# Differential attention in a four-layer kernel: mixing a head's two attention maps before the transpose instead of mixing its two outputs after the product with the values

## The reference, cut to what matters

```python
def diff_attention(h, cos, sin, w_qkv, q_norm, k_norm, lam_p, subln, w_o, layer_idx):
    ...
    lam = jnp.exp(jnp.sum(lp[0] * lp[1])) - jnp.exp(jnp.sum(lp[2] * lp[3])) + lambda_init
    ...
        s = jnp.einsum('bqhcd,bkhcd->bhcqk', qblk, k).astype(jnp.float32) * scale
        causal = kpos[None, :] <= qpos[:, None]
        p = jax.nn.softmax(jnp.where(causal, s, NEG_INF), axis=-1)
        a = p[:, :, 0] - lam * p[:, :, 1]
        return jnp.einsum('bhqk,bkhe->bqhe', a.astype(v.dtype), v)
    ...
    o = rms_norm_2(o, subln) * (1.0 - lambda_init)
    return o.reshape(B, S, DA_V) @ w_o
```

## Time and profile before

| what | value |
|---|---|
| timed runs, median | 1524.88 us (1522.94 to 1527.48) |
| profiled execution | 1526.05 us |
| its span in the trace | 1524.3 us |
| mean granted clock of TensorE, 1 is 2.4 GHz | 0.981 |
| PE busy | 1437.7 us, 94% of the span |
| DVE busy | 939.1 us, 62% |
| ACT busy | 741.4 us, 49% |
| third mixer's attention, first scores to first product of the output projection | 980.07 to 1014.53 us |

### The profile page before, as it was taken

How to read it: one execution, slowest core, us unless ns; L and a number is a source line. 1 busy time by engine, 2 the same in 40 slices (tenths; PEclk the granted TensorE clock), 3 DMA queues, 4 the chain that set the end, 5 groups by cost and what they waited for, 6 DMA issues and landing times.

```text
span 1524.3 us, 19988 instructions
## 1 busy us (share of the span) xinstructions
PE 1437.7 (94%) x7838; PEld 1222.0 (80%) x7838; DVE 939.1 (62%) x1653; ACT 741.4 (49%) x1252; POOL 17.2 (1%) x43
## 2 busy tenths in 40 slices
PE   2889989898999999999999999999999998999998
PEld 2878979887888888888888878778888876888887
DVE  3766666675665554675655559977555487565553
ACT  4734352433444444554545446655444365554441
POOL 2200000000000000000000000000000000000000
PEclk9999999999999999999999999999999997999999
DMA  7413222220456555452665545406655551165552
GB/s 215 111 42 84 83 70 70 69 71 29 142 168 201 181 192 181 147 170 83 200 187 182 191 156 176 166 15 208 190 182 189 186 172 62 56 208 186 187 189 88
DMA packets 168092, 216.60 MB, mean 142 GB/s; under 512 B 10993, under 2 KB 136256, under 8 KB 167872
## 3 DMA queue, kind: packets, MB, share of 16 engines
q1 hardware_dynamic: 166816, 213.03, 43.6%
q10 hardware_dynamic: 1184, 2.31, 0.4%
HBM read 214.26 MB, written 1.05 MB: 141 GB/s over the span
## 4 chain that ended last, share of the span: by engine, by line
PE 84%; DVE 10%; ACT 2%; DMA 2%; issue 1%; POOL 1%; ACTq 0%; SPq 0%; DVEq 0%; POOLq 0%
PE psum L881 22%; PE psum L883 22%; PE psum L882 22%; PE psum L1116 3%; PE psum L1111 2%; DVE w_low L628 2%; PE psum L1227 2%; PE psum L1069 2%; PE psum L1203 2%; DVE work L2187 1%; PE psum L1164 1%; PE psum L1051 1%; DMA ring<-in_gdn_w_in 1%; PE psum L1216 1%; PE psum L661 1%
## 5 line engine op out<-in xcount | busy, mean ns | idle before, releaser
L628 DVE TENSOR_TENSOR w_low<-ring,w_high 128x1024 fp32r<-128x1024 f32 (+3 forms) x395 | 473.7, 1210 | 341.5 <-ACT w_high L614 339.8
L614 ACT ACTIVATE w_high<-ring 128x1024 fp32r<-128x1024 f32 (+3 forms) x395 | 410.6, 1049 | 460.4 <-PE psum L883 443.7
L881 PE MATMUL psum<-w_high,hT 128*128 128x512 f32 (+2 forms) x944 | 373.0, 395 | 0.6 <-DVE hT L1997 0.6
L883 PE MATMUL psum<-w_high,hT 128*128 128x512 f32 (+2 forms) x944 | 367.1, 389 | 0.0
L882 PE MATMUL psum<-w_low,hT 128*128 128x512 f32 (+2 forms) x944 | 366.4, 388 | 0.0
L881 PE MATMUL psum<-w_high,parts 128*128 128x512 f32 (+1 forms) x532 | 208.2, 391 | 1.3 <-ACT arena L1681 1.3
L883 PEld LDWEIGHTS psum<-w_high,hT 128*128 128x128 f32 x944 | 177.8, 188 | 36.8
L883 PE MATMUL psum<-w_high,parts 128*128 128x512 f32 (+1 forms) x532 | 206.2, 388 | 0.0
L881 PEld LDWEIGHTS psum<-w_high,hT 128*128 128x128 f32 x944 | 178.2, 189 | 34.8 <-DVE hT L1997 0.9
L882 PE MATMUL psum<-w_low,parts 128*128 128x512 f32 (+1 forms) x532 | 206.0, 387 | 0.0
L882 PEld LDWEIGHTS psum<-w_low,hT 128*128 128x128 f32 x944 | 178.3, 189 | 34.1
(11 more groups left out here) (278 smaller groups left out, 1541.0 us busy)
## 6 DMA issues: line engine op xcount, KB each, us to landing
ring<-in_ffn_w_gate_up SPq DMA_DIRECT2D x176, 256.0 KB, 3.1
ring<-in_w_gate_up SPq DMA_DIRECT2D x176, 256.0 KB, 3.1
ring<-in_gdn_w_in SPq DMA_DIRECT2D x48, 512.0 KB, 4.0
ring<-in_ffn_w_down SPq DMA_DIRECT2D x44, 512.0 KB, 3.2
ring<-in_w_down SPq DMA_DIRECT2D x44, 512.0 KB, 3.2
ring<-in_da_w_qkv SPq DMA_DIRECT2D x24, 512.0 KB, 3.8
ring<-in_gdn_w_out SPq DMA_DIRECT2D x16, 512.0 KB, 3.3
ring<-in_mla_w_out SPq DMA_DIRECT2D x8, 512.0 KB, 3.9
```

Of the source, the lines that this page charges most:

```text
L614: nc.scalar.activation(piece_slot(w_high, n), piece_slot(ring, n), ACT.Copy).then_inc(s.w_hi, 1)
L628: nc.vector.tensor_tensor(piece_slot(w_low, n), piece_slot(ring, n), piece_slot(w_high, n).bitcast(F32), ALU.subtract).then_inc(s.w_lo, 1)
L881: mm(out, lhs[0], rhs[0], start=start, stop=False)
L883: return mm(out, lhs[1], rhs[0], start=False, stop=stop)
```

## The change

The two maps of a head are combined before they are turned. With `e0`, `e1` the exponentials and `s0`, `s1` their row sums, DVE writes `e0 + (-lambda * s0 / s1) * e1` over `e0`. PE turns that one map (three transposes in place of six) and multiplies it by the values once (three products of width 128 in place of six of width 129). DVE scales the output by `1 / s0`. The row sums no longer come from a column of ones; they are accumulated by the exponentials on ACT (`accum_out`).

The order changes too. On PE a round is: scores of `i + 2` (which wait for the exponentials of `i`), transposes of `i` (which wait for the new signal `mixed`), values of `i - 1`. Transposes alternate between banks 4 and 5, outputs between banks 6 and 7, so `values(i)` waits for the end of round `i - 2`. On ACT a round is: exponentials of `i + 1`, one copy of the turned map, then the squares of head `i - 2` (the piece's `split_high` in round 0). On DVE: `mix(i)`, maxima of `i + 2`, `finished(i - 1)`; `split_low` stands in front of `mix(1)` and `output_norm(0)` in front of `mix(6)`. For heads 0 to 5 the squares are one instruction without a sum, and `output_norm` sums them on DVE: heads 0 to 3 in one reduction over 128x1024, heads 4 and 5 in one over 128x512.

```diff
             def difference_attention(A, q, k, v, outs):      # PE, new
+                def values(i):
+                    if i >= 2:
+                        pe.wait_ge(A.end, i - 1)
+                    pe.wait_ge(A.pT, i + 1)
+                    for t in range(T):
+                        for kt in range(t + 1):
+                            last = mm(B[6 + i % 2][:, t * P:(t + 1) * P], at_pT[:, i % 2, (t + kt) * P:(t + kt + 1) * P], v(i, kt),
+                                      start=(kt == 0), stop=(kt == t))
+                    last.then_inc(A.o_psum, 1)
...
+                for i in range(A.rounds):
+                    if i + 2 < A.rounds:
+                        pe.wait_ge(A.exps, 2 * i + 2)
+                        masked_scores(A, q, k, i + 2)
+                    elif i == A.rounds - 1:
+                        turned_out(0)
+                        turned_out(1)
+                    pe.wait_ge(A.mixed, i + 1)
+                    if i >= 2:
+                        pe.wait_ge(A.pT, i - 1)
+                    for n in range(3):
+                        last = nc.tensor.transpose(B[4 + i % 2][:, n * P:(n + 1) * P], at_s[:, i % 2, 0, n * P:(n + 1) * P], ident)
+                    last.then_inc(A.pT_psum, 1)
+                    if i:
+                        values(i - 1)
+                values(A.rounds - 1)
...
+            def difference_attention(A):                     # ACT, new
...
+                            last = f(at_s[:, u, j, keys_of(t)], B[2 * u + j][:, keys_of(t)], ACT.Exp, scale=A.scale,
+                                     bias=nmax[u][:, t, j:j + 1], accum_out=esum[u][:, t, j:j + 1])
...
+                exps(0)
+                for i in range(A.rounds):
+                    if i + 1 < A.rounds:
+                        exps(i + 1)
+                    act.wait_ge(A.pT_psum, i + 1)
+                    if i >= 2:
+                        act.wait_ge(A.o_psum, i - 1)
+                    f(at_pT[:, i % 2, :], B[4 + i % 2][:, 0:3 * P], ACT.Copy).then_inc(A.pT, 1)
+                    if i == 0:
+                        split_high(act, a_da + 23 + SPLIT)
+                    elif i >= 2:
+                        output_squares(i - 2)
...
-            v.memset(d_v[:, :, :, P:P + 1], 1.0)
...
-            def da_write(i, outs, e):
-                own(ts(e[:, :, 1], e[:, :, 1], lam[:, 3:4], None, ALU.mult))
-                own.wait()
-                own(tt(at_maps, outs, per_map(e, P), ALU.mult))
-                own.wait()
-                return tt(at_o[:, :, i * P:(i + 1) * P], at_maps[:, :, 0, :], at_maps[:, :, 1, :], ALU.add)
             def output_norm(b):
...
+                dve.wait_ge(s.out_sq, 4 if b == 0 else 6)
...
+                own(v.reduce_sum(by_head_t, da_sq[:, summed, :, :].rearrange("p h t n -> p t h n"), AX_X))
+                own.wait()
...
+            def difference_attention(A, turned):             # DVE, new
+                def mix(i):
+                    u = i % 2
+                    dve.wait_ge(A.exps, 2 * i + 2)
+                    if i >= 4:
+                        dve.wait_ge(A.end, i - 3)
+                    own(v.reciprocal(parts_of[i % 4], esum[u]))
+                    own.wait()
+                    own(stt(shares[u], esum[u][:, :, 0], lam[:, 3:4], parts_of[i % 4][:, :, 1], ALU.mult, ALU.mult))
+                    own.wait()
+                    for t in range(T):
+                        first, other = (at_s[:, u, j, keys_of(t)] for j in range(2))
+                        last = stt(first, other, shares[u][:, t:t + 1], first, ALU.mult, ALU.add)
+                    last.then_inc(A.mixed, 1)
+
+                def finished(i):
+                    dve.wait_ge(A.o_psum, i + 1)
+                    tt(at_o[:, :, i * P:(i + 1) * P], B[6 + i % 2][:, 0:T * P].rearrange("p (t n) -> p t n", t=T),
+                       parts_of[i % 4][:, :, 0:1].to_broadcast([P, T, P]), ALU.mult).then_inc(A.end, 1)
+
+                scaled_maxima(A, 0)
+                scaled_maxima(A, 1)
+                for i in range(A.rounds):
+                    if i == 1:
+                        split_low(dve, a_da + 23 + SPLIT)
+                    elif i == 6:
+                        output_norm(0)
+                    mix(i)
+                    if i + 2 < A.rounds:
+                        scaled_maxima(A, i + 2)
+                    elif i == A.rounds - 1:
+                        empty_bank(dve, turned, 0, 0)
+                    if i:
+                        finished(i - 1)
+                finished(A.rounds - 1)
+                empty_bank(dve, turned, 1, 0)
+                output_norm(1)
+                empty_banks(dve, turned, 0, 2)
```

## The result

The changed kernel takes 1530.02 us (median of 11 executions, 1526.51 to 1532.67) against 1523.6 us (11 executions, 1520.9 to 1527.48) for the kernel before. The ratio is 1.0036, 95% interval 1.0025 to 1.0046: slower, by 3.8 to 7.0 us. The profiled execution took 1532.67 us with a span of 1530.7.

A forecast was written before the change was run, and what follows sets the result against it. PE taken as the bound, busy 94%. Stage +0.9 us at high clock, +9.8 at low; less 0.9 in the projection 8.9, adjusted to 8.5: 1534.5 us profiled, 1533 timed; range 1521.5 to 1538.

The forecast's parts named there:

- A: Third mixer's attention: clock falls to 0.50 at the start, middle rounds take 4.4 us each; +8.5 us, chance 0.45.
- rival B: Third mixer: clock returns during the rounds, half at 4.4 us, half at 2.9, second loss later; +5 us, chance 0.2.
- transposes 5 at 990.9 + 4 x 4.4: Third mixer's middle rounds: four rounds at the low clock, 4.4 us each, putting these transposes at 1008.5.
- The round of 2.9 us from a loop: Middle rounds at high clock: mix, transposes, values and finished in a loop set 2.9 us, against 3.54 before.
- `mix` 1.22 us: DVE, each round: reciprocal, two-column product and two three-operand instructions, 1.22 us until it signals.
- The accumulation: ACT's four exponentials now accumulate row sums: 0 to 0.8 us more a round, taken as 0.4.
- The wait in front of transposes 1: Stage start: PE idles 2.6 us for `mix(1)`, which stands behind the `split_low` piece in DVE's queue.
- The norm: `output_norm(0)` in front of `mix(6)`: 4.8 us on DVE, PE idle behind it for 6.6 us.
- The whole sum for the high clock: Third mixer's stage with no clock loss: both ends eat the six rounds' gain, +0.9 us.
- C: Third mixer: clock lost only behind the 6.6 us gap near the end, rounds at high clock; +3 us, chance 0.17.
- D: Fourth mixer: its low stretch, shifted, keeps 2.4 GHz, 6 to 8 us less; chance 0.1.
- E: Fourth mixer: clock comes back later than 1289.4, three rounds at 2.9 us more, 1542 us; chance 0.08.

## Why the prediction was right, and which term was mis-sized

The direction was right and the time inside the range; but the case called likeliest (A, +8.5, 1531 to 1536) didn't happen. What the trace shows is rival B (+5, chance 0.2): the clock comes back during the rounds and is lost a second time behind the norm, and the stage is 4.76 us longer. That the timed difference, 6.4 us, lies nearer to the middle between the two is no support for A; in the profiled executions 2.4 us lie in front of the stage. The forecast's times against the trace, as distances from the first scores:

| place | forecast, high clock | forecast, low clock | measured |
|---|---|---|---|
| scores 2 | 4.68 | 4.68 | 4.93 |
| transposes 1 | 10.43 | 10.83 | 11.15 |
| transposes 5 | 22.03 | 28.43 | 24.56 |
| transposes 6 | 29.68 | 37.03 | 32.25 |
| projection | 35.33 | 44.23 | 39.22 |

- The term that was mis-sized is "transposes 5 at 990.9 + 4 x 4.4", four rounds at the low clock, 17.6 us. They took 13.41 (993.58 to 1006.99): 4.52, 3.17, 2.86, 2.86. The price of a low round was right (4.52 for the one that ran at it from end to end) and their number wrong. This is 4.2 of the 5.0 us by which the low-clock projection time was too late; a further 0.9 is the finishing and the norm behind transposes 5, which were costed at low-clock PE time and ran at the high one (7.69 us measured, 8.6 and 7.65 forecast). The argument for it was the fourth mixer, where 13.6 us of busy PE did not bring the clock back. That stage's stretch stayed at 0.50 after the change too: the window below begins soon behind the stage's first scores and still has waits in it, and from 1282.13 to 1295.73, as far behind the first scores as the row of before, PE is busy for all 13.60 us at 0.50. So the row was no accident; it was just no measure for rounds of other products. Why these rounds brought it back and those did not is open. The runs show only that with the weight piece moved it was back at about 987, with PE busy since 982.63; that in another kernel with the same start it was back at about 994.7, with PE busy since 986.69; and that here it came back between 998 and 999, with PE busy since the second wait.

```profile
1275.40:1289.00 13.60, 11.32 (x56) 7.93 (x56) 9.85 (x30) 6.17 (x17) 0.00 (x0) 0.50 0.39 128
```

(Columns: us, busy us and instructions of PE, PEld, DVE, ACT and POOL, then the clock, DMA share and GB/s.)

- The round of 2.9 us from a loop: 2.86 measured, with a wait of 0.15 for `mix` in each. The run with the outputs finished later supports the loop as the limit: without it every other round is 2.60.
- `mix` 1.22 us: 1.22. Its small steps start 0.03 to 0.04 us behind the end of the one before (992.31 + 0.17 to 992.52), as the earlier trace rows gave it. The 256-column half: 0.48.
- The accumulation, 0.10 us each from the square's row: 0.09. The four exponentials take 1.59 from start to start (985.50 to 987.09), where the forecast adds up 1.65, a term that its row (1.36) and its price (0.4) don't give. The wait in front of scores 2 was forecast at 1.6 us and is 1.88; 0.21 of the difference is that the first maxima start 1.81 us behind the first scores in place of 1.60, behind a copy of the stage before.
- The wait in front of transposes 1, forecast at 2.6 us, is 1.38, because the scores before it ran at the low clock and filled part of it; their start (11.15) is 0.3 us from the forecast. The two runs with the weight piece moved show what that term was worth in all: 3.49 and 2.30 us of stage, where the forecast had named the piece only as one link in a chain.
- The norm: 4.8 us on DVE and 6.6 on PE forecast, 4.82 and 6.47 measured, and the clock lost behind it.
- The whole sum for the high clock, +0.9 us: the kernel with all waits filled has +1.07.
- The 0.9 us that the projection got back: 0.8.
- Rivals C and D: the clock was lost at the start, and the fourth mixer's stage kept its length (43.05 against 42.97), so neither happened. E didn't either. In all twelve kernels the fourth mixer's stage took 42.7 to 43.9 us.

Left open is a part of the timed differences. The kernels whose stage in the trace is shortest gained less in time than there: 0.35 us where the distance to the fourth mixer is 2.64 shorter (286.77 to 284.13), 1.44 where it is 3.89 shorter (to 282.88). The stretch in front of the stage, the same code in all twelve kernels, ended between 975.80 and 984.05 us in their profiled executions, while from the fourth mixer's first scores to the end all took 257.1 to 258.3 us. So one trace can't settle two microseconds of a whole run. The timed differences lie between 1.4 us below and 2.6 above those of the traces' distances from the third mixer's first scores to the fourth's, the changed kernel's 2.4 above (6.4 against 3.97); a cost of the change in front of its stage is neither shown nor ruled out.

## What to carry to other kernels

When an edit shortens rounds, add up both ends at the same time: here the rounds went from 3.54 to 2.86 us, and one piece of other work in front of the first long dependency (3.49 and 2.30 us in two pairs of traces) and one block of small steps in front of a late one ate it all. Put such work where the engine already waits, in parts: with its sums on ScalarE, the end of the stage took 13.79 us with the norm in one piece and 11.82 with its root cut in two between rounds. And price a wait on TensorE with the clock that it costs behind it; a row at the low level tells what a round costs there, but not for how many rounds.

## What was not expected of the hardware

- Needless fp32 transposes of the identity hold 2.4 GHz: 14 in 1.70 us and 20 in 2.35 us kept the clock at 1.00 where the same waits, empty, lost it; in the stage that was worth 2.65 us, and 3.69 with the gap of the norm filled too (52 in 5.84 us, clock 1.00).
- In the gap of the norm the granted clock stays at 1.00 for most of the time in which PE does nothing (window 1009 to 1012: busy 0.00, clock 1.00) and falls only at its end; the work behind it runs at 0.50.
